# State input matmuls paired by row group with real and imaginary steps apart, and one state output step for four tiles, in a hybrid encoder layer

## The reference, cut to what matters

```
lam_bar = exp(lam * step)
bu = einsum('blgc,gpc->blgp', u, b_bar)                # state input, complex
if h0: bu[:, 0] += lam_bar * h0                        # the sample rows have a start state
h  = associative_scan(a * h + bu)                      # h_t = lam_bar * h_{t-1} + bu_t
y  = einsum('blgp,gcp->blgc', h, c).real + d_skip * u  # state output
z  = gelu(y);  out = z * sigmoid(z @ w_glu + b_glu)
```

## Time and profile before

| | us |
|---|---|
| runs | 1729.95, 1732.47, 1731.99; median 1731.99 |
| profiled execution, its own time | 1731.17 |
| its span in the trace | 1729.5 |
| eight chunks (lines 995 to 1131) | about 36 to 396 of the span |
| experts | about 640 to 1700 of the span |

### The profile page before, as it was taken

How to read it: one execution, slowest core, us unless ns; L and a number is a source line. 1 busy time by engine, 2 the same in 40 slices (tenths; PEclk the granted TensorE clock), 3 DMA queues, 4 the chain that set the end, 5 groups by cost and what they waited for, 6 DMA issues and landing times.

```text
span 1729.5 us, 22987 instructions
## 1 busy us (share of the span) xinstructions
PE 1528.1 (88%) x8908; PEld 993.5 (57%) x8908; DVE 571.0 (33%) x1022; ACT 139.7 (8%) x294; POOL 227.3 (13%) x366
## 2 busy tenths in 40 slices
PE   5999999999999899998898898898888887889775
PEld 3777777777777775564454455454454544545433
DVE  6998888874110421111111102101101101111115
ACT  3011111113000300000000000000000000000001
POOL 3666666600000010000000000000000000000003
PEclk9999999999999769999999999999999999999997
DMA  7554544533586049999999999999999999999974
GB/s 178 131 150 114 136 127 119 137 107 85 163 286 219 26 170 410 408 417 405 415 412 407 417 412 408 408 417 416 389 417 416 389 416 415 415 410 412 417 262 167
DMA packets 175314, 520.04 MB, mean 301 GB/s; under 512 B 23504, under 2 KB 135248, under 8 KB 147952
## 3 DMA queue, kind: packets, MB, share of 16 engines
q1 hardware_dynamic: 160032, 485.73, 73.1%
q10 hardware_dynamic: 13056, 17.77, 3.2%
q0 software_dynamic: 2128, 15.21, 3.1%
HBM read 496.72 MB, written 21.95 MB: 300 GB/s over the span
## 4 chain that ended last, share of the span: by engine, by line
PE 42%; DMA 41%; DVE 9%; issue 4%; SPq 1%; ACT 1%; POOL 1%; DVEq 0%; POOLq 0%; ACTq 0%
DMA e_ring<-in_w_exp_up_dram 34%; PE bank L995 12%; PE bank L1343 11%; DMA e_ring<-in_w_exp_gate_dram 7%; PE bank L1362 3%; PE bank L1285 3%; PE bank L1215 2%; PE bank L1320 2%; PE bank L1145 2%; DVE e_ring L1526 2%; SPq L576 1%; PE bank L1037 1%; PE bank L1029 1%; DVE e_ring L1530 1%; PE bank L1006 1%
## 5 line engine op out<-in xcount | busy, mean ns | idle before, releaser
L1343 PE MATMUL bank<-e_ring,xT_exp 128*64 128x256 f32 x4096 | 477.0, 390 | 101.8 <-DMA e_ring<-in_w_exp_gate_dram 60.8
L1343 PEld LDWEIGHTS bank<-e_ring,xT_exp 128*64 128x64 f32 x4096 | 295.2, 140 | 293.7 <-DMA e_ring<-in_w_exp_gate_dram 81.7
L1362 PE MATMUL bank<-e_ring,hidT 128*64 128x512 f32 x1024 | 244.4, 633 | 38.7 <-DVE hidT L1847 38.7
L995 PE MATMUL bank<-xT,w_ring 128*128 128x288 f32 x1024 | 258.6, 411 | 0.7 <-issue 0.7
L995 PEld LDWEIGHTS bank<-xT,w_ring 128*128 128x128 f32 x1024 | 193.5, 191 | 57.1 <-issue 5.1
L1842 DVE TENSOR_TENSOR hid<-bank,sig_exp 128x256 f32<-128x256 f32 x32 | 13.6, 424 | 562.9 <-ACT sig_exp L947 562.9
L1362 PEld LDWEIGHTS bank<-e_ring,hidT 128*64 128x64 f32 x1024 | 74.7, 145 | 186.3 <-issue 141.5
L746 POOL DMA_INDIRECT e_ring<-expert_rows_out,idx x6 | 5.5, 925 | 1073.4 <-ACT all_stored_mark L756 1071.9
L1285 PE MATMUL bank<-hT,w_ring 128*128 128x288 f32 (+2 forms) x640 | 136.2, 373 | 0.0
L1285 PEld LDWEIGHTS bank<-hT,w_ring 128*128 128x128 f32 x640 | 111.4, 192 | 19.2
L1853 DVE COPY rows<-bank 128x512 f32<-128x512 f32 x32 | 22.1, 692 | 238.8 <-PE bank L1362 238.8
(11 more groups left out here) (306 smaller groups left out, 1228.9 us busy)
## 6 DMA issues: line engine op xcount, KB each, us to landing
e_ring<-in_w_exp_gate_dram SPq DMA_DIRECT2D x64, 2048.0 KB, 27.3
e_ring<-in_w_exp_up_dram SPq DMA_DIRECT2D x64, 2048.0 KB, 28.0
e_ring<-in_w_exp_down_dram SPq DMA_DIRECT2D x64, 2048.0 KB, 22.4
w_ring<-in_w_in_dram SPq DMA_DIRECT2D x32, 1024.0 KB, 6.2
w_ring<-in_w_out_dram SPq DMA_DIRECT2D x16, 1024.0 KB, 6.6
w_ring<-in_w_ple_gate_dram SPq DMA_DIRECT2D x16, 1024.0 KB, 23.6
expert_rows_out<-hT POOLq DMA_DIRECT2D x3, 1536.0 KB, 9.5
w_ring<-in_ssm_w_glu_dram SPq DMA_DIRECT2D x4, 1024.0 KB, 5.2
```

Source lines behind the costliest of these rows:

```text
L995: last_mm = pe.matmul(out, weights(k), moving[:, k, :], start=(k == 0), stop=(k == n - 1))
L1343: mm = pe.matmul(gu[h * B:(h + 1) * B, s % 2, :], xT_exp[:, c, s // 2, :], w[:, c, h * FH:(h + 1) * FH], start=(s == 0 and c == 0), stop=( ...
L1362: mm = pe.matmul(bank[h * B:(h + 1) * B, 3 + n, :], hidT[:, c, half, :], e_ring[:, 2 * (NGU + half) + c, h * DH2 + n * 512:h * DH2 + (n + ...
```

## The change: what it does

`bu(c, p, r)` now does one part (r = 0 real, 1 imaginary) of two tiles 2p and 2p+1: two matmuls from different 32-row groups, one into bank 2 and one into bank 3. There are still four such calls in a chunk. The real call of a pair keeps a place between projections: `bu(c, 0, 0)` where `bu(c, 0)` was, `bu(c, 1, 0)` where `bu(c, 2)` was. The imaginary call is issued inside the next projection, ahead of its sixth of 16 matmuls, through `between` in `dense`: that of pair 0 in `proj(c, 1)`, that of pair 1 in `proj(c, 3)`. `y_out` does the four tiles in one call of eight matmuls, after `proj(c + 1, 0)`. VectorE works in `pair`: two products of the real parts, two of the imaginary parts, and then the rest of tile 2p and of tile 2p+1; the attention weights come after the rest of tile 0. Two tiles of scratch are added, and `mask_s` and `tmp3` lie elsewhere in the same memory.

```
@@ -216,6 +216,7 @@
         ysig = early(T)
         tmp1 = early(2, T)
         tmp2 = early(2, T)
+        tmp4 = early(2, T)
         rot = early(2, T)
         scan = early(2, T)
         h_ssm = early(JC, 2, T)
@@ -242,7 +243,6 @@
         wgt = early(ZW)
         wT = early(480)
         mask = early(P + TP)
-        mask_s = early(PAST + TS)
         par_c = early(7, JC)
         d_c = early(1)
         last = early(2, 2, NJ)
@@ -302,6 +302,8 @@
         v_rows = carve(e_flat, (P,), tail)[0:nvec, :]
         pr = carve(e_flat, (18, P), tail)[0:NJ]
         p_rows = carve(e_flat, (NT, PLC * P), tail)
+        tmp3 = carve(e_flat, (2, T), tail)
+        mask_s = carve(e_flat, (PAST + TS,), tail)
         zeros_x = hT[:].rearrange("p k t -> p (k t)")[0:B, 2048:2048 + D]
         assert used[0] <= 10 * D, used
 
@@ -990,8 +992,10 @@
 
         @block.tensor
         def _(pe):
-            def dense(out, weights, moving, n):
+            def dense(out, weights, moving, n, between=None):
                 for k in range(n):
+                    if k == 5 and between is not None:
+                        between()
                     last_mm = pe.matmul(out, weights(k), moving[:, k, :], start=(k == 0), stop=(k == n - 1))
                 return last_mm
 
@@ -1014,26 +1018,27 @@
             pe.wait_ge(xt_odd, KC // 2)
             pe.wait_ge(par_copied, 1)
 
-            def proj(c, s, first):
+            def proj(c, s, first, between=None):
 
                 pe.wait_ge(w_landed[s], c * 16 + 16)
                 if not (first and s < 2):
                     pe.wait_ge(proj_copied, c * 4 + s - 1)
                 w = w_ring[:, s, :].rearrange("p (k n) -> p k n", n=P)
-                dense(bank[:, s % 2, 0:T], lambda k: w[:, k, :], xT, KC).then_inc(dense_done, 1)
-
-            def bu(c, i, first):
-                if not (first and i == 0):
-                    pe.wait_ge(bu_used, c * JC + i)
+                dense(bank[:, s % 2, 0:T], lambda k: w[:, k, :], xT, KC, between).then_inc(dense_done, 1)
+
+            def bu(c, p, r, first):
+                if not (first and p == 0 and r == 0):
+                    pe.wait_ge(bu_used, c * JC + 2 * p + r)
+                for q in range(2):
+                    i = 2 * p + q
+                    mm = pe.matmul(bank[:, 2 + q, 0:T], bcT[32 * i:32 * i + 32, r, :], uT[32 * i:32 * i + 32, :], start=True, stop=True)
+                mm.then_inc(bu_ready, 1)
+
+            def y_out(c):
+
+                pe.wait_ge(h_ready, c * JC + JC)
                 for r in range(2):
-                    mm = pe.matmul(bank[:, 2 + r, 0:T], bcT[32 * i:32 * i + 32, r, :], uT[32 * i:32 * i + 32, :], start=True, stop=True)
-                mm.then_inc(bu_ready, 1)
-
-            def y_out(c, h):
-
-                pe.wait_ge(h_ready, c * JC + 2 * h + 2)
-                for r in range(2):
-                    for i in (2 * h, 2 * h + 1):
+                    for i in range(JC):
                         mm = pe.matmul(bank[32 * i:32 * i + 32, 4, 0:T], bcT[:, 2 + r, 32 * i:32 * i + 32], h_ssm[:, i, r, :],
                                        start=(r == 0), stop=(r == 1))
                 mm.then_inc(y_part, 1)
@@ -1045,7 +1050,9 @@
                     glu_start(0)
                     glu_start(1)
                 if prev:
-                    y_out(c - 1, 1)
+                    if not first:
+                        pe.wait_ge(y_read, c - 1)
+                    y_out(c - 1)
                 if cur:
 
                     pe.wait_ge(bc_ready, c + 1)
@@ -1072,7 +1079,7 @@
                 if cur:
                     pe.wait_ge(proj_copied, c * 4 + 1)
                     pe.wait_ge(bcT_copied, c + 1)
-                    bu(c, 0, not prev)
+                    bu(c, 0, 0, not prev)
                 if prev:
                     if not cur:
                         pe.wait_ge(ckT_copied, c)
@@ -1082,14 +1089,13 @@
                 if not cur:
                     glu_start(2)
                 if cur:
-                    proj(c, 1, not prev)
+                    proj(c, 1, not prev, lambda: bu(c, 0, 1, False))
                     pe.wait_ge(ck_landed, c * 16 + 16)
                     if prev:
                         pe.wait_ge(kn_copied, c * 2)
                     for t in range(2):
                         mm = pe.transpose(bank[:, 7, t * P:(t + 1) * P], ck[:, t, :], ident[:])
                     mm.then_inc(ckT_ready, 1)
-                    bu(c, 1, False)
                     proj(c, 2, not prev)
                 if prev:
 
@@ -1101,7 +1107,7 @@
                         mm = pe.transpose(bank[0:m, 7, t * P:(t + 1) * P], vT[:, t0:t0 + m], ident[:])
                     mm.then_inc(vn_ready, 1)
                 if cur:
-                    bu(c, 2, False)
+                    bu(c, 1, 0, False)
                 if prev:
                     pe.wait_ge(wgt_ready, c)
                     pe.transpose(bank[:, 5, 0:P], wgt[:, 0:P], ident[:])
@@ -1111,11 +1117,7 @@
                     pe.transpose(bank[:, 5, 416:448], wgt[0:TS, Z2 + P:Z2 + 2 * P], ident[0:TS, 0:TS])
                     pe.transpose(bank[0:TS, 5, 448:480], wgt[0:TS, Z2 + PAST:ZW], ident[0:TS, 0:TS]).then_inc(wT_ready, 1)
                 if cur:
-                    proj(c, 3, not prev)
-                    bu(c, 3, False)
-                    if prev:
-                        pe.wait_ge(y_read, c)
-                    y_out(c, 0)
+                    proj(c, 3, not prev, lambda: bu(c, 1, 1, False))
                 if not cur:
                     for m in range(4):
                         glu_rest(m)
@@ -1508,34 +1510,42 @@
                 dve.tensor_scalar(xT[:, k, :], bank[:, k % 4, 0:T], vecT[:, a:a + 1], vecT[:, b:b + 1],
                                   ALU.mult, ALU.add).then_inc(xt_odd, 1)
 
-            def tile(c, i, first):
-
-                n = c * JC + i
+            def pair(c, p, first, between):
+
+                n = c * JC + 2 * p
                 cb = 0 if first else c % 2
-                w = tb[:, ds(cb, 1), :, i, :].rearrange("p b r t -> p (b r) t")
-                wre, wim = (w[:, r:r + 1, :].to_broadcast([P, 2, T]) for r in range(2))
-                dve.wait_ge(bu_ready, n + 1)
-                own(dve.tensor_tensor(tmp1, bank[:, 2:4, 0:T], wre, ALU.mult))
-                dve.tensor_tensor(tmp2, bank[:, 2:4, 0:T], wim, ALU.mult).then_inc(bu_used, 1)
-                dve.wait_ge(bu_used, n + 1)
-                own(dve.tensor_tensor(rot[:, 0, :], tmp1[:, 0, :], tmp2[:, 1, :], ALU.add))
-                own(dve.tensor_tensor(rot[:, 1, :], tmp1[:, 1, :], tmp2[:, 0, :], ALU.subtract))
+                w = [tb[:, ds(cb, 1), :, 2 * p + q, :].rearrange("p b r t -> p (b r) t") for q in range(2)]
+                by_re, by_im = (tmp1, tmp3), (tmp2, tmp4)
+                for r, out in enumerate((by_re, by_im)):
+                    dve.wait_ge(bu_ready, n + r + 1)
+                    own(dve.tensor_tensor(out[0], bank[:, 2:3, 0:T].to_broadcast([P, 2, T]), w[0], ALU.mult))
+                    dve.tensor_tensor(out[1], bank[:, 3:4, 0:T].to_broadcast([P, 2, T]), w[1], ALU.mult).then_inc(bu_used, 1)
+                dve.wait_ge(bu_used, n + 2)
                 own.wait()
-                for r in range(2):
-                    for a, b, start in ((0, TP, 0.0), (TP, T, par_c[:, 5 + r, i:i + 1])):
-                        own(dve.tensor_tensor_scan(scan[:, r, a:b], par_c[:, 0, i:i + 1].to_broadcast([P, b - a]),
-                                                   rot[:, r, a:b], start, ALU.mult, ALU.add))
-                own.wait()
-                own(dve.tensor_tensor(tmp1, scan, wre, ALU.mult))
-                own(dve.tensor_tensor(tmp2, scan, wim, ALU.mult))
-                own.wait()
-                if not first:
-                    dve.wait_ge(y_part, c * 2 - 1 + i // 2)
-                own(dve.tensor_tensor(h_ssm[:, i, 0, :], tmp1[:, 0, :], tmp2[:, 1, :], ALU.subtract))
-                dve.tensor_tensor(h_ssm[:, i, 1, :], tmp1[:, 1, :], tmp2[:, 0, :], ALU.add).then_inc(h_ready, 1)
-                dve.wait_ge(h_ready, n + 1)
-                dve.tensor_copy(last[:, :, :, ds(n, 1)].rearrange("p r t j -> p r (t j)"),
-                                h_ssm[:, i, :, TP - 1:T:TS]).then_inc(last_ready, 1)
+                for q in range(2):
+                    i = 2 * p + q
+                    wre, wim = (w[q][:, r:r + 1, :].to_broadcast([P, 2, T]) for r in range(2))
+                    a, b = by_re[q], by_im[q]
+                    own(dve.tensor_tensor(rot[:, 0, :], a[:, 0, :], b[:, 1, :], ALU.add))
+                    own(dve.tensor_tensor(rot[:, 1, :], b[:, 0, :], a[:, 1, :], ALU.subtract))
+                    own.wait()
+                    for r in range(2):
+                        for t0, t1, start in ((0, TP, 0.0), (TP, T, par_c[:, 5 + r, i:i + 1])):
+                            own(dve.tensor_tensor_scan(scan[:, r, t0:t1], par_c[:, 0, i:i + 1].to_broadcast([P, t1 - t0]),
```

(58 more changed lines are left out.)

## The result

The changed kernel takes 1779.2 us (median of 4 runs, 1777.46 to 1780.02) against 1731.42 (4 runs): ratio 1.0275, 95% interval 1.0257 to 1.0293. Forecast were 1776.7 us, 1758 to 1795. The profiled execution took 1779.07 us with a span of 1777.4.

A forecast was written before the change was run, and what follows sets the result against it. The prediction took a chain of waits through VectorE, not TensorE's busy time, to bound the chunks. 43.5 us (chunks 1 to 6) + 3.3 - 2.1 = +44.7 on 1731.17 gave 1775.9, 1776.7 as a median, range 1758 to 1795.

The forecast's parts named there:

- Two legs per period: Chunks 1 to 6: a VectorE leg from scores to freeing the banks, then a TensorE leg of 14.77 us.
- State input pair 0.66: New state input: its two matmuls in different row groups overlap, taking 0.66 us instead of 1.16.
- Rival 3: State input: row groups do not overlap, 1783.2 us in all; chance 0.25 together with rivals 2 and 4.
- TensorE's leg +4.0: Chunks 1 to 6, from the freeing to the next state input: 18.75 us against 14.77, 11 projection matmuls behind the wait.
- VectorE's leg +1.55: Chunks 1 to 6: the freeing of the banks moves from 162.40 to about 163.95, 0.95 hand-over plus 0.6 GpSimd slowing.
- hand-over: Pair 0: VectorE waits for TensorE's imaginary state input between real and imaginary products, 0.95 us.
- rival 2: Chunks 1 to 6: GpSimd and VectorE exclude each other in full, 3.6 us more, 1780.3; chance 0.25 with rivals 3 and 4.
- Clock 1.7 a chunk: Behind the 8.4 us wait in projection 3, TensorE's clock halves for 3.4 us, losing 1.7; bounds 0 and 2.7.
- Rival 1: Clock stays high or its low stretch ends before TensorE resumes: 11.9 us less, 1764.8; chance 0.20.
- rival 4: Low clock behind the wait lasts 5.4 us: 7 x 1.0 us more, 1783.7; chance 0.25 with rivals 2 and 3.
- Chunk 0 +3.3, chunk 7 -2.1: Chunk 0 loses 3.3 us to a wait in projection 3; chunk 7, without a table, gains 2.1 from TensorE's savings.
- rival 5: VectorE frees the banks before TensorE needs them: 28.5 us gained, 1703.5; chance 0.04.

The follow-up runs named there:

- E4: The changed kernel without GpSimd's tables of powers for chunks 2 to 7, only the first step of each left: 1718.31 us, ratio 0.9913.
- E3: The kernel before without GpSimd's tables of powers for chunks 2 to 7, only the first step of each left: 1728.23 us, ratio 0.9975.
- E8: The changed kernel with pair 1's imaginary state input ahead of the eleventh matmul of projection 3 instead of the sixth: 1748.88 us, ratio 1.0099.
- E2: The changed kernel with filler matmuls in chunks 0 to 6, 7 ahead of the attention-weights wait, 10 ahead of pair 1's imaginary state input: 1761.89 us.
- E1: The changed kernel with the imaginary state input of pair 1 moved behind projection 3 instead of inside it: 1763.95 us, ratio 1.0180.
- E7: E1 with 7 filler matmuls ahead of the wait for the attention weights in chunks 1 to 6: 1754.68 us, ratio 1.0130.
- E5: The kernel before with only the state output of four tiles in one call behind the next projection 0: 1730.85 us, ratio 0.9987.

## Why the prediction was right, point by point

- **Two legs per period.** Right, and the base of the rest: the saved matmuls (TensorE's work fell by 2.9 us a chunk in E4 against E3; 3.0 was said) did not shorten a period that VectorE ends.
- **State input pair 0.66.** 0.69 us from start to next start (142.74 to 143.43): row groups run side by side. Rival 3 falls, and so does the estimate of 0.82 that the prediction worked out from the factor for four tiles in the Trainium skill (TensorE: Matmul & The Clock Gate, Part 3); the measurement decides. State output of four: 1.10 (191.37 to 192.47), with 1.2 said.
- **TensorE's leg +4.0.** It grew by 5.4, of which E8 and E2 give 1.7 to the clock: 3.7. The state output never waited, as said. The sum of the terms for VectorE's last tile is 13.05, not the 13.5 written; it took 12.2 (174.08 to 186.30), so nothing hangs on it.
- **VectorE's leg +1.55.** +1.47. The hand-over is 0.86 with 0.95 said; the rest is GpSimd's, 0.6. The sum came out, the picture in between did not: I had the attention weights ready before TensorE needs them, and they are 3.1 us late. So one sign that I had named, TensorE idle for 7 to 9 us inside `proj(c, 3)`, is there in chunk 1 alone. The length of the leg did not suffer, as the wait for the weights only came out of the later one (2.0 instead of 8.4), but in E1 it held up all of projection 3. A sum over a leg does not say which instruction in it is slowed.
- **GpSimd and VectorE exclude each other in full (rival 2).** Between: 0.6 of at most 1.2 us. The rows speak for GpSimd having used the time at the start, when VectorE read PSUM: it came to its first step of 128 elements 4.3 us after the start of the table instead of 7.0, and ended it 24.9 us into the period instead of 27.8. A total over three sections does not show whether two single instructions exclude each other in full; no run was made for it.
- **Clock 1.7 a chunk.** The size is right in five chunks of seven by E2 (1.65 to 2.0 in chunks 0, 2, 3, 4 and 6), and the way to it is in part luck. The prediction argued from one wait of 8.4 us with a low stretch of 3.4 behind it. In chunks 2, 3, 4 and 6 the late weights had cut the wait in two, and it is a wait of 2.0 to 2.4 us that a low stretch of 3.4 follows. Where one long wait did come, in chunk 1, the clock was low for 6.5 us of work and cost 3.1, more than the upper bound of 2.7; chunk 5 lost 3.3. In all 15.1 us with 11.9 said. Rival 1 falls; rival 4 (2.7 a chunk) is wrong for five chunks and near for two.
- **Chunk 0 +3.3, chunk 7 -2.1.** From the first state input +3.0, and -2.2.
- **Sum +44.7 in the chunks.** +45.5. Here too errors cancel: chunks 2, 3, 4 and 6 grew by 6.9 us with 7.25 said, chunk 1 by 8.4 and chunk 5 by 8.6. That the median is 2.5 us above the forecast is within what the expert stage scatters.
- **Faster (rival 5).** E4 shows its condition: with the tables gone the banks are free in time and the change gains 9.7 us in the chunks over the kernel before without tables (E3). The price of 28.5 us, against the kernel before, was too high: E4's eight chunks are 15.1 us shorter than those (347.9 to 332.9). The hand-over at pair 0, which it left out, takes 1.0 of the 3.9 a period, and chunk 0, beside which the table of chunk 1 is still made, loses 4.1 in the place of gaining 3.0.

What is not settled: the 21 us that E7 keeps are divided above by reading one chunk, not by an experiment; an order on VectorE with the weights ahead of the rest of tile 0 was not tried.

## What to carry to other kernels

Before moving an operation that waits into the middle of a long accumulation, count what is queued behind it on its engine: here half a microsecond per matmul, 11 of them, in seven chunks. A saving on an engine that is busy for 98% of a stage is worth little while another engine ends its period (0.27 of 1.1 us in E5); the chain of waits showed that where the busy shares did not. A wait of 2 us on TensorE can cost its length and then 1.7 us more in clock. And a forecast that comes out can hold a term that is right for the wrong reason: go through the signs one by one, as here the idle time of 7 to 9 us that did not come.

## What the runs showed of the hardware that was not expected

The low clock came back behind short waits: after 3.08 us of waiting in chunk 2 the granted clock is 0.51 for the whole 6.3 us of work that follows, and a second low stretch follows a wait of only 2.0 us. Filler matmuls that do nothing took both away. The same wait does not always do it: of ten waits of 1.95 to 2.05 us ahead of the state output in chunks 2 to 6 of E1 and E7, four were followed by the low clock. The kernel before had shown as much among its experts, where 11 of 13 waits of 2.2 us were followed by it, this one for example (the granted clock is 0.53 over 3.2 us from its first matmul on):

```profile
843.36 8.58 PE L1362 MATMUL bank<-e_ring,hidT 128*64 128x512 f32 x32 [2.22 <-DVE hidT L1847]
```

GpSimd's table takes 22.0 us from its first step to its last when its small steps meet VectorE reading PSUM (145.66 to 167.65), and 24.9 when they meet VectorE reading SBUF (135.44 to 160.29), at the same instructions.
